# Key projections by the seven-product scheme through DRAM, pooling averages on VectorE, modulation chunks under the value units

## The reference, cut to what matters

```
h = rmsnorm(x) * (1 + scale1) + shift1          # mod = silu(c) @ w_mod + b_mod, 6 x 1024
q, k, v, o, gates, u_pool, g_a, g_b = h @ w_in + b_in
y_a = mLSTM(q, k / sqrt(128), v, gates)         # 8 heads of 128, forward and backward
y_b = (mean over a window of u - u) @ w_pool    # 4 groups, windows 2, 4, 8, 16
                                                # 1-D for context, w x w for latent
x = x + gate1 * ((sig(g_a) * (y_a @ Wa) + sig(g_b) * (y_b @ Wb)) @ w_out)
x = x + gate2 * moe(rmsnorm(x) * (1 + scale2) + shift2)
```

## Time and profile before

| | us |
|---|---|
| median of 3 runs (range) | 963.46 (962.69 to 963.84) |
| the profiled execution, its time | 961.65 |
| its span, first to last instruction | 959.8 |
| TensorE matmul busy | 935.3 (97%) |
| VectorE busy | 706.0 (74%) |
| ScalarE busy | 489.0 (51%) |
| GpSimd busy | 136.0 (14%) |
| mean granted TensorE clock | 0.992 |

### The profile page before, as it was taken

The page is one execution under the profiler, slowest core; times in us unless marked ns, Lnnn a source line. Parts: engine busy times, 40 slices in busy tenths (PEclk is TensorE's granted clock), DMA queues, the critical chain, the costliest instruction groups (busy, mean ns, idle before and its releaser), DMA issues.

```text
span 959.8 us, 14248 instructions
## 1 busy us (share of the span) xinstructions
PE 935.3 (97%) x5618; PEld 829.0 (86%) x5618; DVE 706.0 (74%) x922; ACT 489.0 (51%) x651; POOL 136.0 (14%) x141
## 2 busy tenths in 40 slices
PE   7999999999999999999999999989999999999986
PEld 5799999978788999999999988868888888888862
DVE  5798777559223488989454546369999999999998
ACT  5565442131312456666311232247787887887763
POOL 0000000199910101001000000020112111111100
PEclk9999999999999999999999999979999999999999
DMA  9814442288671343335382155159999999999964
GB/s 371 343 44 134 150 131 103 80 305 313 236 298 73 99 144 100 94 122 200 109 328 88 45 209 208 45 204 408 421 419 405 424 420 414 414 416 413 395 275 162
DMA packets 39634, 229.39 MB, mean 239 GB/s; under 512 B 4336, under 2 KB 4784, under 8 KB 19088
## 3 DMA queue, kind: packets, MB, share of 16 engines
q1 hardware_dynamic: 26928, 180.12, 47.8%
q0 software_dynamic: 10048, 41.70, 12.2%
q10 hardware_dynamic: 2592, 6.66, 1.8%
HBM read 205.81 MB, written 22.66 MB: 238 GB/s over the span
## 4 chain that ended last, share of the span: by engine, by line
PE 91%; DMA 4%; DVE 3%; issue 1%; SPq 0%; ACT 0%; DVEq 0%; POOLq 0%; ACTq 0%
PE ps L1984 85%; PE ps L2042 2%; DMA raw<-in_wst 1%; PE ps L2516 1%; DMA h2scr<-ht 1%; PE ps L2544 1%; PE ps L2031 1%; PE ps L2358 0%; DMA xg<-h2scr,slot_rows 0%; PE ps L2259 0%; DVE rowA L1939 0%; DVE xr L1942 0%; DVE xr L1946 0%; PE ps L2435 0%; DMA rowB<-yscr 0%
## 5 line engine op out<-in xcount | busy, mean ns | idle before, releaser
L706 ACT ACTIVATE whi<-raw 128x2048 fp32r<-128x2048 f32 x18 | 34.4, 1911 | 95.9 <-PE ps L1984 63.4
L1984 PE MATMUL ps<-hhi,whi 128*128 128x320 f32 x352 | 81.2, 312 | 0.0
L1984 PE MATMUL ps<-hhi,wlo 128*128 128x320 f32 x352 | 80.2, 309 | 0.0
L1984 PE MATMUL ps<-hlo,whi 128*128 128x320 f32 x352 | 78.9, 309 | 0.0
L1795 DVE TENSOR_TENSOR olo<-raw,ohi 128x2048 fp32r<-128x2048 f32 x32 | 72.4, 2289 | 3.9 <-ACT ohi L1073 3.9
L1795 DVE TENSOR_TENSOR wlo<-raw,whi 128x2048 fp32r<-128x2048 f32 x31 | 70.3, 2290 | 5.3 <-ACT whi L1073 4.7
L1169 DVE TENSOR_TENSOR wlo<-raw,whi 128x2048 fp32r<-128x2048 f32 x18 | 41.9, 2327 | 40.4 <-ACT whi L706 40.4
L1073 ACT ACTIVATE whi<-raw 128x2048 fp32r<-128x2048 f32 x32 | 61.3, 1918 | 18.9 <-PE ps L1984 18.9
L1073 ACT ACTIVATE ohi<-raw 128x2048 fp32r<-128x2048 f32 x32 | 61.3, 1918 | 18.0 <-PE ps L1984 18.0
L1984 PEld LDWEIGHTS ps<-hhi,whi 128*128 128x128 f32 x352 | 58.6, 188 | 6.2 <-issue 4.2
L1984 PEld LDWEIGHTS ps<-hhi,wlo 128*128 128x128 f32 x352 | 58.8, 188 | 0.0
(11 more groups left out here) (429 smaller groups left out, 2574.8 us busy)
## 6 DMA issues: line engine op xcount, KB each, us to landing
raw<-in_wexp SPq DMA_DIRECT2D x64, 1024.0 KB, 9.2
raw<-in_wst SPq DMA_DIRECT2D x59, 1024.0 KB, 6.2
eraw<-in_wexp SPq DMA_DIRECT2D x32, 1024.0 KB, 8.6
nm<-negscr POOLq DMA_DIRECT2D x8, 640.0 KB, 7.0
wib<-wiscr POOLq DMA_DIRECT2D x8, 512.0 KB, 6.1
thscr<-gout ACTq DMA_DIRECT2D x12, 320.0 KB, 4.8
TH<-thscr POOLq DMA_DIRECT2D x3, 1280.0 KB, 7.8
xT<-in_x SPq DMA_DIRECT2D x4, 640.0 KB, 6.0
```

What stands on the lines that cost most here:

```text
L706: act.activation(dst[:, :], raw[raw_slot(c)][:, :], ACT.Copy).then_inc(hi_ready, 1)
L1984: return nc.tensor.matmul(out, lhsT, rhs, start=start, stop=stop)
```

## The change

- Pairs: ten become fourteen (`SPILLS` = gate pairs and key pairs, then queries). A key block is combined in `gout`, scaled and biased by ScalarE (`finish_block`), and spilled to `thscr`. `block_k` goes, with `q_ready`, `q_free`, `q_used`.
- GpSimd reads the keys back (`keys_back`): head 0 when the pairs have ended, heads 1 to 5 when `U` has been stored, heads 6 and 7 after the first load of `wib` and the second of `nm`.
- The four averages run on VectorE (`averages`), one in the gate arithmetic, one behind it, two behind the last value chunk's split. GpSimd only loads the counts and clears the pads of window g + 1 when `s_avg` says that window g is done, then stores `U`. The averages' tiles move to 134.5 to 148 KB and some small places; `vb`, `mst` and `mrows` move too.
- The 16 chunks of the second modulation stand one behind each of the first 14 value units and two behind the fifteenth; the chunk order of the stream is changed to match (`V_AT`).
- `gate_rows` follows value unit (2, 3), the second turn (3, 0), the transpose of `mst` (3, 2). `mod_add(1)` and the making of `mst` (`mod_rows`) follow both late averages and two output-gate splits on VectorE. `mask_maxima(0)` stands between the third and fourth value row of the second half.

```diff
+            def keys_back(a, b):
+                gp.dma_start(QK[:, H + a:H + b, :], thscr[2 * N_GE + a:2 * N_GE + b, :, :].rearrange(
+                    "f p t -> p f t")).then_inc(d_pool, 16)
+
+            keys_back(0, 1)
+            gp.memset(Vt[:, :, :, DH:V1], 1.0).then_inc(s_init, 1)
+            for g in range(NG):
+                if g:
+                    gp.wait_ge(s_avg, g)
+                gp.dma_start(rcnt_l[:, :], rcnt_d[:, g, TC:T]).then_inc(d_pool, 16)
+                gp.dma_start(rcnt_c[:, :], rcnt_d[:, g, 0:TC]).then_inc(d_pool, 16)
+                for pad in (XP[0][:, :, :], RP[0][:, :, :], CP[0][:, :]):
+                    gp.memset(pad, 0.0).then_inc(s_pads, 1)
+            gp.wait_ge(s_avg, NG)
             gp.dma_start(uscr, U[:, :, :]).then_inc(d_pool, 16)
+            gp.wait_ge(d_pool, D_U)
+            keys_back(1, H - 2)
             gp.wait_ge(d_rows, 32)
             gp.wait_ge(s_modT, KT + 2)
...
             load_maxima(1)
+            gp.wait_ge(d_pool, D_KEYS[0])
+            keys_back(H - 2, H)
...
+            def averages(g):
+                w = WIN[g]
+                dve.wait_ge(u_out, g + 1)
+                dve.wait_ge(s_pads, 3 * g + 3)
+                ul = U[:, g, TC:T].rearrange("p (r c) -> p r c", c=GW)
+                st.on(dve.tensor_copy(CP[0][:, PAD:PAD + TC], U[:, g, 0:TC]))
+                st.do(dve.tensor_copy(XP[0][:, :, PAD:PAD + GW], ul))
+                n, s, src = GW + 2 * PAD, 1, 0
+                m = TC + 2 * PAD
+                while s < w:
+                    n -= s
+                    m -= s
+                    st.on(dve.tensor_tensor(CP[1 - src][:, 0:m], CP[src][:, 0:m],
+                                            CP[src][:, s:s + m], ALU.add))
+                    st.do(dve.tensor_tensor(XP[1 - src][:, :, 0:n], XP[src][:, :, 0:n],
+                                            XP[src][:, :, s:s + n], ALU.add))
+                    s, src = 2 * s, 1 - src
...
+                dve.wait_ge(d_pool, D_RCNT[g])
+                st.on(dve.tensor_tensor(CP[1 - src][:, 0:TC], cs, rcnt_c[:, :], ALU.mult))
...
+                dve.tensor_tensor(ul, mean_l, ul, ALU.subtract).then_inc(s_avg, 1)
...
             pick(gF[:, :], gA[:, :], gB[:, :])
-            splits_lo(1)
+            averages(0)
+            split_lo(v_at(2), QH[0], QL[0])
...
+            averages(1)
+            mod_add(0)
             dve.wait_ge(d_const, 32)
             dve.wait_ge(s_init, 2)
+            for t in range(NT):
+                value_rows(0, t)
+            split_lo(v_at(3), QH[1], QL[1])
+            averages(2)
+            averages(3)
...
             gate_lo(0)
             gate_lo(1)
+            mod_add(1)
+            mod_rows()
             dve.wait_ge(s_gt, 3)
             dve.wait_ge(d_late, 32)
+            for t in range(3):
+                value_rows(1, t)
             mask_maxima(0)
-            for t in range(NT):
+            for t in range(3, NT):
                 value_rows(1, t)
...
+            MOD2_AFTER = {divmod(i, NT): i for i in range(N_MOD2 - 1)}
             for c in range(N_V):
                 for t in range(NT):
                     value_block(c, t)
-                    if c == 0 and t == 2:
+                    at = MOD2_AFTER.get((c, t))
+                    if at is not None:
+                        if at == KT:
+                            mod2_turned(0)
+                        mod2_product(at)
+                        if at == N_MOD2 - 2:
+                            mod2_product(at + 1)
+                    if (c, t) == (2, 3):
+                        gate_rows()
+                    if (c, t) == (3, 0):
                         mod2_turned(1)
...
-            pe.wait_ge(q_free, 3 + 2 * N_K)
+            pe.wait_ge(g_cmb, PRODUCTS * PAIRS)
+            pe.wait_ge(d_pool, D_U)
             pe.wait_ge(v_free, 6 + 6)
```

More of the change, by code:

```diff
@@ L424, in layer_kernel @@
             "g_sum", "g_hi", "g_lo", "g_mm", "g_cmb", "g_ev", "u_ready", "u_out"))
-        SPILLED = 16 + 16 * N_GE
+        SPILLED = 16 + 16 * SPILLS
+        D_RCNT = [16 + 32 * (g + 1) for g in range(NG)]
+        D_U = D_RCNT[-1] + 16
+        D_KEYS = D_U + 16, D_U + 32
+        D_U2, D_ZERO = D_U + 48, D_U + 64
         block = ctx.enter_context(nc.Block())
@@ L532, in _ @@
             gp.wait_ge(g_mm, PRODUCTS * PAIRS)
+            gp.wait_ge(g_cmb, PRODUCTS * PAIRS)
             gp.memset(gOne[:, :], 1.0).then_inc(s_init, 1)
[L534 to L584, removed]
@@ L585, in _ @@
-            gp.sem_inc(s_pool, 1)
+            for b in range(2):
+                gp.wait_ge(d_tile[b], SPILLED)
+            def keys_back(a, b):
[10 more added lines that the diff above has]
+                    gp.memset(pad, 0.0).then_inc(s_pads, 1)
@@ L834, in mod_row2 @@
                 act.activation(mrow[:, :], ps[:, 6, :], ACT.Copy).then_inc(s_mrow, 1)
[L836 to L851, removed]
+            act.wait_ge(g_mm, PRODUCTS * PAIRS)
+            split_hi(v_at(1), QH[1])
+            log_sigmoid()
+            act.wait_ge(v_ready, NT)
+            split_hi(v_at(2), QH[0])
+            mod_row2(0)
             act.wait_ge(s_gt, 1)
@@ L1368, in _ @@
+            split_lo(v_at(1), QH[1], QL[1])
             dve.wait_ge(s_gate, 5)
@@ L1436, in _ @@
                .then_inc(s_gt, 1)
-            for j in range(2, N_K):
-                splits_lo(j)
-            split_lo(AT_V + 1, QH[1], QL[1])
-            mod_add(1)
-            dve.wait_ge(m_done, 2)
-            dve.wait_ge(d_pool, 16 * (NG + 1))
-            for v, b in ((2, 24), (3, 40)):
-                st.on(dve.tensor_copy(mst[:, v, :, :], mod[:, b:b + KT, :].rearrange("p k c -> p c k")))
-            st.on(dve.tensor_scalar(mst[:, 0, :, :], mod[:, 16:24, :].rearrange("p k c -> p c k"), 0.5,
-                                    None, ALU.mult))
-            st.on(dve.scalar_tensor_tensor(mst[:, 1, :, :], mod[:, 32:40, :].rearrange(
-                "p k c -> p c k"), 1.0, by(col[:, G_2:G_2 + KT].unsqueeze(1), [P, 2, KT]),
-                ALU.add, ALU.mult))
-            st.wait()
-            dve.sem_inc(s_mst, 1)
             def value_rows(g, t):
@@ L2175, in _ @@
                 product(j, 6, 6, *b22)
-            def block_k(j, b):
-                e = 2 * j + b
-                if b == 0:
-                    chunk_split(k_at(j))
-                pe.wait_ge(q_free, e + 1)
-                for k in range(KT):
-                    o = (b * KT + k) * P
-                    last = three([(ps[:, KEY_BANK[e % 3] + a, 0:HALF], cut_half(a)) for a in range(2)],
-                                 QH[j % 2][:, o:o + P], QL[j % 2][:, o:o + P], hhi[:, k, :], hlo[:, k, :],
-                                 k == 0, k == KT - 1)
-                last.then_inc(q_ready, 1)
             def mod2_turned(g):
-                pe.wait_ge(m_done, g)
+                if g:
+                    pe.wait_ge(m_done, g)
+                    pe.wait_ge(s_gt, 3)
                 pe.wait_ge(s_mrow, KT + 1 + g)
@@ L2668, in _layout @@
     wm2 = wm2.reshape(-1, P, CH)
-    keys = [wq[N_Q, 0]]
-    for n in range(N_MOD2):
-        if n % 4 == 2:
-            keys.append(wq[N_Q + n // 4 + 1, 0] if n < N_MOD2 - 2 else wv[0])
-        keys.append(wm2[n])
+    values = []
+    for n in range(N_V):
+        values += [wv[n]] + list(wm2[V_AT[n] - n:(V_AT + (N_V + N_MOD2,))[n + 1] - n - 1])
     wu0 = wu[:1].reshape(1, P, 2, KT, P).transpose(0, 1, 3, 2, 4).reshape(1, P, CH)
-    wst = np.concatenate([wu0, wm1, wu[1:], wl[N_O:N_O + N_GE], wq[:N_Q, 0], keys, wv[1:],
+    wst = np.concatenate([wu0, wm1, wu[1:], wl[N_O:N_O + N_GE], wq[N_Q:, 0], wq[:N_Q, 0], values,
                           wl[:N_O], wl[N_O + N_GE:],
```

200 lines of the change are left out of this document (103 added, 97 removed).

## The result

The changed kernel takes 969.34 us (median of 6, 965.43 to 972.50), the kernel before 963.58 (6, 960.94 to 963.92): ratio 1.0058, 95% interval 1.0036 to 1.0080. It is slower by 5.8 us (3.5 to 7.7 by the interval). I had forecast slower, 973.0 against 963.46, which is 9.5; the range of 963.5 to 981 holds the result.

What follows compares the result with a forecast made beforehand. TensorE's issue order was taken as the clock before the change; afterwards VectorE's averages and the loads behind them hold Q. Profiled 961.65 + 7.5 (Q later) + 2.0 (clock) = 971.2, plus 1.8 to the median: 973.0 us, range 963.5 to 981.

Steps and rivals of the forecast that it cites:

- TensorE's own gain: Keys and second modulation on TensorE: 7.0 us from fewer products, 2.3 given back by seven more switches, 4.7 gained.
- Q: Start of the first output-gate quarter behind the first scores, 320.4 before; forecast at T0 + 90.4, 7.5 us slower.
- VectorE's queue: Splits, gates, value rows and four averages in order on VectorE from T0; last average forecast to end 71.4 us later.
- T0: End of the last pair product, 188.2 in the trace before; forecast 49.3 us later with the four extra pairs.
- The pads' wait: VectorE idle before the fourth average until GpSimd has cleared its pads: 3.2 us.
- The two waits of TensorE on the way: Under the values, unit 11 waits 2.6 us for value rows, unit 17 1.5 for modulation rows; a later wait swallows both.
- From s to Q: Store of U, keys, head 0's maxima queued behind them, mask, exponentials, score copy: 19.0 us; TensorE idle about 9.
- s: End of the last average on VectorE, forecast at T0 + 71.4.
- The clock: TensorE's clock falls to the lower level in the idle before Q: between 0 and 5 us, taken as 2.
- All cover holds: Rival: averages quicker or maxima early, Q comes with TensorE, 958.8 us; break-even is s at 63.9; 9%.
- GpSimd was not what slowed the gate instructions: Rival: VectorE's gate instructions stay slow with GpSimd idle, VectorE 12.2 us later at s, 985 us; 7%.
- The stream binds: Rival: the stream of chunks delays the values beyond what the wait before Q hides, 978 with 5 us more; 7%.

Runs made afterwards that it cites:

- delay_3us: The changed kernel with three dummy additions of 960 columns (3.5 us) on VectorE ahead of the third average: 973.03 us, ratio 1.0112 to the kernel before.
- store_in_two: The changed kernel, head 0's maxima loaded first, three quarters of U stored before the fourth average, one output-gate chunk held until the states land: 959.22 us, ratio 0.9969.
- third_chunk_early: The changed kernel with the third value chunk one position earlier in the stream: 968.98 us, ratio 1.0070 to the kernel before.
- gpsimd_busy: The changed kernel with 20 additions of 128x256 on GpSimd beside the second half of the gates: 975.42 us, ratio 1.0131 to the kernel before.
- maxima_before_keys: The changed kernel with loads behind the store of U reordered to head 0's maxima, states, then keys of heads 1 to 5: 966.52 us, ratio 1.0034.
- doubles: The changed kernel with the modulation chunks in twos behind eight value units: 969.36 us, ratio 1.0077 to the kernel before.
- maxima_first: The changed kernel with GpSimd's queue behind the averages reordered: head 0's maxima, store of U, states, keys of heads 1 to 5: 965.0 us, ratio 1.0018.
- keep_clock: The changed kernel with 14 dummy products on TensorE between the second and third score of head 0: 966.82 us, ratio 1.0044 to the kernel before.

## Why the prediction was right in sign and 3.7 us too high

The chain that I forecast, last average, store, keys, maxima, mask, exponentials, score copy, is the one in the trace, and delay_3us shows it one for one. The sizes of its terms were off.

- *TensorE's own gain: right.* 4.7 us in the sum; Q with the wait removed (store_in_two) comes 4.7 earlier. The pairs end at 237.1 (said 237.5), a lone chunk costs 3.95 - 2.72 = 1.23 (said 1.18). Two bounds beside that sum are wrong: with a full 2.04 for a lone chunk the loss is 7.3 us, not 5.9, and the gain of 7.0 belongs to a lone chunk at half of a double, 1.02; at the 0.86 of its weight loads alone it would be 9.3.
- *VectorE's queue, the step that was mis-sized.* The last average ends at T0 + 66.3, not 71.4: the 5.1 us that matter. I put the two 16x640 instructions and the log-sigmoid behind the second split, as in the trace before; in the changed queue they stand ahead of it, and ScalarE was done 0.5 us after the split. The first split ends at T0 + 9.4 as counted, the subtraction starts at 9.9, not 13.9: 4.0. The averages sum to 27.7, not 29.4: 1.7. They are 4.7, 6.6, 8.9 and 7.55; a one-source copy of 512 columns takes 0.42, the lower end that I gave it. The gates are 1.7 shorter in their two halves, and 0.6 lies in joins and value rows. Against these 8.0 stands a wait that I hadn't: 2.98 for the third chunk, which took 9.0 us from issue to landing. That the two partly cancel is luck; third_chunk_early, where that wait is 0.61, ends the averages 2.0 earlier.
- *The pads' wait: right*, 3.1 for 3.2. *The two waits of TensorE on the way* (2.6 and 1.5) did not come, since VectorE was 4 to 5 us ahead; with VectorE later they are there: 1.7 at the transpose of the modulation rows in delay_3us, 4.4 at the value rows in gpsimd_busy.
- *From s to Q: 20.15, said 19.0.* The wait for the store was 4.96, the keys were issued at s + 5.8 (said 5.6), the maxima landed at s + 15.0 (said 14.2): they came 8.3 us after an issue that stood 0.8 behind that of the keys. maxima_before_keys shows the queueing, 4.9 without it. From their landing to Q it was 5.2 (said 4.8).
- *The clock: 2.3, said 2.* It fell to the lower level in the wait (0.58 in 318 to 321) and came back between 327 and 330. The Trainium skill, TensorE: Matmul & The Clock Gate, "Why this matters for your kernels", has it that a gap spent waiting for DMA brings the engine back to the lower level. This trace agrees, with a wait of 7.8 us. In maxima_before_keys' profiled execution it did not hold, with 3.5 us of idle time at 1.00.
- *The fit for the load.* By the Trainium skill, DMA: Bandwidth & Descriptors, "Anatomy of one DMA", the 1600 KB of keys would take an estimated 5.8 us. By the row I had counted 7.0. They took 7.5, with the maxima, the states and a chunk in flight beside them. The rows were nearer.
- *The sum by what was measured*: -5.1 at s, +1.15 to Q, -0.4 at T0 and +0.3 of clock are -4.0; 9.5 - 4.0 = 5.5 against 5.8 measured.
- *The rivals.* "All cover holds" did not come: s missed its break-even, T0 + 63.9, by 2.4 us as counted, and with s to Q as measured the break-even is T0 + 62.8. Of what spoke for it the fast copies came true; the absence of queueing did not, and what brought it near was mostly the log-sigmoid, which I had not named. Its 9% was low. *GpSimd was not what slowed the gate instructions* falls: beside an idle GpSimd they took 10.1 us, beside a busy one 15.0. The stream binds only a little: 1.2 us on TensorE in doubles, 2.0 at s in third_chunk_early, of which 0.6 reaches Q. The added 1.8 us from the profiled execution to the median was right for the kernel before only: the changed kernel's profiled execution (969.60) is its median (969.34), since two stages behind 600 us were slower in it.
- *What would show it.* None of the signs of being wrong came: TensorE took 9.9 us from the first scores to Q, the averages sum to 27.7, the maxima landed at 318.4 (forecast near 323).

## What to carry to other kernels

When work moves into an engine that was slack, follow that engine's queue to the instruction that everyone waits for, and read the order in the new code, not in the old trace. A small load that others wait for goes ahead of a large one on its queue, but with others beside it a large one takes longer (the store of U 8.8 us for 5.2): TensorE's waits before Q were gone only when most of the store was done earlier and a chunk was held back. A saving on the engine that bounds the kernel is found again only when the wait that hides it is gone; here the same pairs came with 5.8 us more or 3.2 less than before, by the order, size and time of a few DMAs.

## What the runs showed of the hardware

- GpSimd's additions made VectorE's short instructions longer: 15.0 against 10.1 us for the same 23, one 16x128 instruction 0.62 against 0.27, and the first 16x640 one 1.23 where none of that kind takes over 0.87 in the changed kernel.
- Waits of 0.8 and 2.1 us shortly behind each other (maxima_first) and one of 2.7 (keep_clock) were followed by the lower clock; one of 3.5 us (maxima_before_keys) and one of 2.0 (store_in_two) were not. The length of the wait alone does not tell it.
- The 640 KB of maxima landed 8.3 us after their issue behind the keys and 4.9 ahead of them, though at the 409 GB/s that the full stream reaches (241 to 273 us) their size is 1.6.
